# Two first weight loads go from SyncE's DMA queue to ScalarE's

## The reference

```python
def _mlstm_branch(x, w_in, conv_w, conv_b, w_q, w_k, w_v, b_i, b_f, norm_g, skip, w_out):
    B, S, _ = x.shape
    H = N_HEADS_A
    proj = x @ w_in
    xm = proj[..., :E_A]
    z = proj[..., E_A:2 * E_A]
    o_pre = proj[..., 2 * E_A:3 * E_A]
...
    xc = jax.nn.silu(_causal_dwconv(xm, conv_w, conv_b))
...
def reference(x, mlstm_w_in, ...):
    for i in range(DEPTH):
...
        x = _layer_norm(DEEPNORM_ALPHA * x + branch, post_ln_g[i], post_ln_b[i])
    return x
```

## Time and profile before

| | |
|---|---|
| median of 3 runs | 1396.07 us |
| lowest and highest | 1395.18 and 1397.42 us |
| profiled execution, its own time | 1395.2 us |
| span of it (first to last instruction) | 1393.4 us |
| TensorE busy | 1380.7 us, 99% |
| VectorE busy | 1160.8 us, 83% |
| ScalarE busy | 765.1 us, 55% |
| mean granted TensorE clock | 0.999 of 2.4 GHz |

### The profile page before, as it was taken

The page is one execution under the profiler, slowest core; times in us unless marked ns, Lnnn a source line. Parts: engine busy times, 40 slices in busy tenths (PEclk is TensorE's granted clock), DMA queues, the critical chain, the costliest instruction groups (busy, mean ns, idle before and its releaser), DMA issues.

```text
span 1393.4 us, 19119 instructions
## 1 busy us (share of the span) xinstructions
PE 1380.7 (99%) x6608; PEld 1156.1 (83%) x6608; DVE 1160.8 (83%) x1883; ACT 765.1 (55%) x1338; POOL 153.8 (11%) x251
## 2 busy tenths in 40 slices
PE   9999999999999999999999999999999999999997
PEld 7888888888888888888888888878888888888886
DVE  7989999898998989899874446797888888899976
ACT  6875766747576675757733436564333333336341
POOL 2002011110101111010000001101111111110021
PEclk9999999999999999999999999999999999999999
DMA  6114334262433525345497767434566555699651
GB/s 230 46 42 137 98 94 142 67 179 65 136 99 87 149 63 168 80 138 174 137 328 249 221 192 226 132 110 114 156 163 159 153 149 153 169 296 335 217 197 76
DMA packets 103439, 213.31 MB, mean 153 GB/s; under 512 B 10912, under 2 KB 27552, under 8 KB 102192
## 3 DMA queue, kind: packets, MB, share of 16 engines
q1 hardware_dynamic: 90544, 178.53, 38.5%
q0 software_dynamic: 12800, 33.56, 12.4%
HBM read 170.04 MB, written 75.56 MB: 176 GB/s over the span
## 4 chain that ended last, share of the span: by engine, by line
PE 95%; DVE 3%; ACT 0%; issue 0%; DMA 0%; POOL 0%; DVEq 0%; SPq 0%; ACTq 0%; POOLq 0%
PE wide L2898 21%; PE wide L2900 20%; PE wide L2899 20%; PE ps_state L2898 3%; PE ps_state L2900 3%; PE ps_state L2899 3%; PE ps_inter L2899 2%; PE ps_inter L2898 2%; PE ps_inter L2900 2%; PE ps_intra L3078 2%; PE ps_s L2898 2%; PE ps_intra L2898 2%; PE ps_intra L2900 2%; PE ps_s L2900 2%; PE ps_s L2899 2%; PE ps_intra L2899 2%
## 5 line engine op out<-in xcount | busy, mean ns | idle before, releaser
L2899 PE MATMUL wide<-xa,inb 128*128 128x512 f32 x576 | 224.7, 390 | 0.0
L2898 PE MATMUL wide<-xb,inb 128*128 128x512 f32 x472 | 189.6, 402 | 0.9 <-DVE inb L1931 0.7
L2900 PE MATMUL wide<-xb,inb 128*128 128x512 f32 x472 | 184.3, 390 | 0.0
L2899 PEld LDWEIGHTS wide<-xa,inb 128*128 128x128 f32 x576 | 108.4, 188 | 20.3
L2899 PE MATMUL wide<-xa,blk 128*128 128x512 f32 x320 | 124.5, 389 | 0.0
L2900 PEld LDWEIGHTS wide<-xb,inb 128*128 128x128 f32 x472 | 88.6, 188 | 19.2
L2898 PEld LDWEIGHTS wide<-xb,inb 128*128 128x128 f32 x472 | 88.8, 188 | 18.7 <-DVE inb L1931 1.1
L2898 PE MATMUL wide<-xb,blk 128*128 128x512 f32 x256 | 99.7, 389 | 0.8 <-ACT zz L1802 0.8
L2900 PE MATMUL wide<-xb,blk 128*128 128x512 f32 x256 | 99.6, 389 | 0.0
L1850 ACT ACTIVATE wy<-wy_raw 128x1024 fp32r<-128x1024 f32 x56 | 59.3, 1061 | 62.2 <-DMA wy_raw<-y_block 61.9
L2898 PE MATMUL wide<-xa,inb 128*128 128x512 f32 x208 | 83.2, 400 | 0.7 <-DVE inb L1931 0.7
(11 more groups left out here) (448 smaller groups left out, 3983.5 us busy)
## 6 DMA issues: line engine op xcount, KB each, us to landing
in_raw<-in_w_in SPq DMA_DIRECT2D x45, 512.0 KB, 4.3
wy_raw<-y_block SPq DMA_DIRECT2D x56, 256.0 KB, 4.5
mw_raw<-h_block SPq DMA_DIRECT2D x53, 256.0 KB, 3.3
m_sum<-in_w_out POOLq DMA_DIRECT2D x48, 256.0 KB, 4.3
h_block<-f_buf SPq DMA_DIRECT2D x48, 256.0 KB, 2.8
w_sum<-in_pool_w_out POOLq DMA_DIRECT2D x48, 256.0 KB, 4.3
a_raw<-in_pool_w_z SPq DMA_DIRECT2D x16, 512.0 KB, 4.1
a_raw<-folded SPq DMA_DIRECT2D x16, 512.0 KB, 4.4
```

The source lines that it names most:

```text
L2898: pe.matmul(dst, a[0], b[0], start=first, stop=False, skip_group_check=more)
L2899: pe.matmul(dst, a[0], b[1], start=False, stop=False, skip_group_check=more)
L2900: return pe.matmul(dst, a[1], b[0], start=False, stop=last, skip_group_check=more)
```

## The change

`load_first` is taken out of SyncE's part, with its two calls between the loads of x. The two same DMAs, with the same source, destination and semaphores, stand on ScalarE ahead of its first work. No wait is added or removed.

```diff
-            def load_first(j):
-                sp.dma_start(in_raw[:, 2 * j, :], p_in[0, :, j, 0, :, :].rearrange("c t f -> c (t f)")
-                             ).then_inc((w_half_in[0], w_lower_in)[j], 16)
-
...
             for t in range(4):
                 load_quadrant(0, x_tile_in[t], t, t + 1)
-                if t < 2:
-                    load_first(t)
             load_quadrant(2, xt_in[2], 0, 2)
...
+            for j in range(2):
+                act.dma_start(in_raw[:, 2 * j, :], p_in[0, :, j, 0, :, :].rearrange("c t f -> c (t f)")
+                              ).then_inc((w_half_in[0], w_lower_in)[j], 16)
             operand_hi(0)
             in_high(0)
             operand_hi(1)
```

## The result

The changed kernel takes 1399.20 us (median of 22 runs, 1396.52 to 1402.85) where the kernel before takes 1395.31 us beside it (22 runs, 1394.20 to 1400.06). I had forecast 1396.4 us and a range up to 1398.2 us. The profiled execution took 1399.2 us, with a span of 1397.4 us against 1393.4 us.

What follows compares the result with a forecast made beforehand. TensorE, busy 1380.7 of 1393.4 us, was taken as the bound, so only its start could shift. The median before, 1396.07 us, plus +0.3 us for a later x tile 0 gave 1396.4 us, range 1394.5 to 1398.2 us.

Steps and rivals of the forecast that it cites:

- What stands on the path: Whole kernel: TensorE, busy 1380.7 of 1393.4 us, bounds it; a change at the start only shifts its whole stream.
- The table load: ScalarE's start: two issues delay its end from 2.00 to 2.94 us, hidden by 2.55 us of idle time.
- W: Start: landing time of the first weights, 6.07 us before and forecast near that; the first product follows 1.54 us later.
- X: Start: landing time of x tile 0, 4.53 us before, forecast between 4.53 and 6.07 us.
- The formula: Start: the first product begins at the later of W + 1.54 and X + 2.17 us.
- Case A: Start: queues share evenly, x tile 0 lands later; 0 to +0.63 us, middle +0.3 us, 1396.4 us; chance 0.42.
- The sum of even sharing: Start: x tile 0 and first weights both land at 6.07 us, first product at 8.24 us, a loss of 0.63 us.
- No case reaches that: Whole time: no case moves it by the detectable 2.8 us; gains capped at 0.86 us; slower given 0.05.
- A change of TensorE's clock is no rival of its own: Start: idle time growing from 0.70 to at most 2.0 us leaves 2.4 GHz, as 2.7 us did at the end.

Runs made afterwards that it cites:

- e1: Changed kernel with 32 transposes at the start in place of 24; +3.2 us (2.0 to 4.6) against the kernel before.
- e3: Kernel before with only weights 0 issued by ScalarE, weights 1 staying on SyncE; -0.1 us (-1.8 to 1.5) against before.
- e12: Changed kernel with 36 transposes at the start in place of 24; +2.4 us (1.3 to 3.6) against the kernel before.
- e11: Changed kernel unaltered, run again on another chip; +2.2 us (1.1 to 3.5) against the kernel before.
- e4: Kernel before with only weights 1 issued by ScalarE, weights 0 staying on SyncE; +1.0 us (-0.7 to 2.5) against before.
- e10: Changed kernel with weights 0 moved to offset 4 KB and weights 1 to 6 KB of their 8 KB rows; -0.6 us (-1.8 to 0.8) against before.
- e8: Changed kernel with each first tile of x and weights in one 256 KB piece of DRAM; -0.4 us (-2.0 to 1.1) against before.
- e9: Kernel before with each first tile of x and weights in one 256 KB piece of DRAM; -0.6 us (-2.0 to 0.8) against before.
- e2: Kernel before with 16 transposes at the start in place of 24; +1.5 us (0.3 to 2.7) against before.
- e13: Kernel before with 28 transposes at the start in place of 24; +0.8 us (-0.7 to 2.2) against before.
- e7: Changed kernel with roles swapped: ScalarE issues x tiles 0 and 1, SyncE the weights; +2.9 us (1.4 to 4.3) against before.
- e5: Kernel before, all on SyncE, order x tile 0, x tile 1, weights 0, weights 1; +1.4 us (-0.3 to 2.9) against before.

## Why the prediction was wrong, point by point

- **What stands on the path: right.** TensorE's stream moved as one; the lag of the gate step lies within the interval of the time for the changed kernel and for 9 of the 12 experiments (not e1, e3 and e12), and no other engine became a bound at the start. The table load stayed hidden: 2.93 us against 2.94 us forecast. Each issue took 0.45 us.
- **"W near 6.07 us as before, X between 4.53 and 6.07 us": nearly.** The weights landed at about 6.1 us, x tile 0 at about 6.3 us (5.7 to 6.3 us in the four profiled executions of this kernel). The formula held: x tile 0 landed at 6.28 us, 6.28 + 2.17 is 8.45 us, and the product started at 8.41 us. Case A was the right mechanism, and its end of +0.63 us was measured as +0.80 us. I took the middle, +0.3 us, for no better reason than that the order wasn't seen. The sum of even sharing, which also followed from the Trainium skill's round-robin rule ("DMA: Bandwidth & Descriptors", section "Queues, rings and completion order"), was the one to take: from 2.3 to 2.6 us this trace has 12 packets in each of the two queues.
- **The step that failed: that a loss can only come through the landing of x tile 0.** "No case reaches that: [...] a loss of 2.8 us would need x tile 0 to land at 8.2 us" takes the first product's two inputs as the whole path, and puts two terms at nothing. x tile 0 landed at 6.3 us, and the stream was still 3.10 us late at the gates. Only 0.80 us of that is the sum that I had; 0.66 us is x tile 1 and 1.60 us the half clock, the two points that follow.
- **x tile 1 was left out.** I followed the first product's two inputs and not the fourth's. Its row was there: x tile 1 was taken at 6.75 us, without idle time, and so had next to nothing to spare. It was issued earlier, but now lands beside weights 1, and was taken 1.7 us later: 0.66 us of TensorE's time. In e11 and e12 it was taken at 7.72 and 7.29 us.
- **"A change of TensorE's clock is no rival of its own": wrong.** At the end of the program 2.7 us of idle time left the clock at 2.4 GHz. At the start it fell to 1.2 GHz for 3 us behind 1.76 us and then 0.50 us of idle time, in this execution; in e11's profiled one, with 1.72 us and then 0.34 us, it didn't. One row from another place is no bound for a gate that falls in some executions and not in others. The price here is 1.60 us, and the changed kernel's lag at the gates less e1's, 3.10 - 1.41 = 1.69 us, says about the same. That is the price in one execution; the medians of e1 and e12 don't show it. The Trainium skill, in "TensorE: Matmul & The Clock Gate", section "Part 1: The HAM clock gate (the "warmup" mystery)", warns that the same kernel changes its clock at different points from run to run, and the traces agree: 24 transposes at the start took between 4.34 and 5.38 us.
- **The size of the scatter.** I widened the range by 0.7 and 0.8 us for the runs, less than the 0.9 and 1.35 us that I had named for it. The late waits alone differ by 3 us between the profiled executions of the table (0.17 to 3.36 us).
- **The rule that spoke against the change** held. It is the Trainium skill's, in "DMA: Bandwidth & Descriptors", section "Issuing engines are not separate DMA queues": more issuers save only the sequencer's time. The rates from 2.0 to 4.6 us agree: 159 GB/s with one queue and 151 GB/s with two, and 298 and 299 GB/s with contiguous tiles. e4 and e10 moved more because of where their weights lie. The rule names no loss, and I took none from it, though sharing is a loss for whoever was first in the one queue.

What stays open: why e1 and e12, whose lag at the gates is 1.4 and 1.2 us, measure 3.2 and 2.4 us; their profiled executions show 3.20 and 2.66 us of late waits, against 0.17 to 3.36 us elsewhere, but one execution of each doesn't tell chance from cause. So 1.2 to 1.8 us of the loss of these two have no cause on record. Why the layout of before is slow wasn't tried further. And whether e8, e9 or e10 beats before can't be said: their ratios are 0.9997, 0.9996 and 0.9996, all with intervals around 1. All three beat the changed kernel as first measured: their intervals end at 1.0008 or lower, and its own begins at 1.0014. Beside its repeat on the same chip (e11, 1.0008 to 1.0025) e10 still does (its interval ends at 1.0006).

## What to carry to other kernels

A load that is put on a second queue takes its share from the load that was first in the one queue, and the rate of both together needn't rise; if the first load is the one that is waited for soonest, that is a loss. Look at where the first loads lie in DRAM before moving an issue: here shifting one of them within its rows, or laying the tiles out in one piece, raised the rate of the first loads by 1.8 times, which the queue didn't. When the start of a kernel is moved, follow every input of the first dozen products, not only the first one's, and count a half clock as possible as soon as the idle time in front grows. Compare rates over a stretch that is long enough: over 0.5 us they misled me, over 2.6 us they agreed between executions. A second issuer saves issue time only, and issue wasn't what anyone waited for here.

## What the runs showed of the hardware

- From 2.0 to 4.6 us, loads of x tile 0 and weights 0, both the first 2 KB of 8 KB rows, moved 159 to 171 GB/s on one queue (before, e2, e13) and 151 to 162 GB/s on two (the changed kernel, e1, e11, e12, e3, e7). With x tile 1 behind x tile 0 on one queue it was 218 GB/s (e5). With weights 4 KB further in on the second queue it was 248 GB/s (e4) and 291 GB/s (e10), with contiguous tiles 298 GB/s on one queue (e9) and 299 GB/s on two (e8).
- A second queue that loads weights 0 delayed the first load of the other: x tile 0 was taken at 5.70 to 6.31 us in place of 4.36 to 4.57 us, and with contiguous tiles at 4.52 us in place of 3.43 us. With the second queue's load 4 KB further in it was taken at 4.69 us (e4) and 4.76 us (e10).
- TensorE's clock fell to 1.2 GHz after 1.76 us and 0.50 us of idle time, after 2.15 us (e2, by the spacing of the products alone), 1.95 us (e3) and 1.40 us with 0.39 us (e7), and not after 1.72 us with 0.34 us (e11) or 1.46 us (e5); it came back about 3 us later. The transposes at the start show it rising at different times as well: 24 of them took 5.38, 5.12, 4.62, 4.55 or 4.34 us in different executions, so the idle time behind them varies by a microsecond although the transposes are the same; in the changed kernel alone they took 5.12 and 4.62 us.
